# Operand placement, narrow projections in one tile, and 512-column units in a two-block forward pass on one core

## The chip, the cores and the metric

The kernel runs on one core of a Trainium2 chip. A core has TensorE (PE, matrix products), VectorE (DVE), ScalarE (ACT), GpSimd (POOL) and SyncE (SP, which here issues the loads); they run side by side and wait for one another through semaphores. The metric is the time of one execution on the device, in microseconds, as the median of several runs.

## The reference

A forward pass over 512 tokens of width 1024 in fp32: two layers of a first block (a mixer with a gated delta rule and HGRN2, then a convolutional FFN), then one layer of a second block (four mixers, one of them sparse attention, with gates, then an MLP). Cut to what this change touches:

```python
def _mixer(h, w_in, ...):                        # twice
    p = h @ w_in                                 # 1024 -> 6672 columns
    (qkv, z, beta_r, a_r, hq, hf_fwd, hf_bwd, hi, hgate, gate_dn, gate_hg) = _split(p, IN_SIZES)
    beta = jax.nn.sigmoid(beta_r) ...            # beta_r, a_r: 8 columns each, a "narrow projection"
    g = -jnp.exp(dn_a_log) * jax.nn.softplus(a_r + dn_dt_bias)
    ...
    for d, fr in enumerate((hf_fwd, hf_bwd)):    # 512 columns each: the decays
        logf = jax.nn.log_sigmoid(fr) + jnp.log1p(lb[d] * jnp.exp(-fr))
        kk = (1.0 - lb[d]) * jax.nn.sigmoid(-fr)
    ...
    return merged @ w_out
# second block, once
    (gu, gv, q, kc, vc, ks_, vs_, kw, vw, ng, ca, cb, sB, sC, sh) = jnp.split(xn @ w_in[l], split_points)
    ...                                          # ng: 12 columns, the other narrow projection
    gates = jax.nn.sigmoid(xn @ w_gate[l] + b_gate[l])
```

## The kernel before, in words

Every large product is made from three fp32r matmuls. An operand x is kept as a high part (x rounded to fp32r by ScalarE, HHI or WHI) and a low part (x minus the high part, HLO or WLO), and `product` adds high x high, low x high and high x low in PSUM for each tile k of 128 rows of the contraction (lines 145 to 147). A matmul loads 128 x 128 stationary elements and moves up to 512 columns past them.

Stages follow each other, each a block with a barrier, an own order written out by hand for each engine and waits on named steps. Per layer of the first block: `qkv_stage`, `delta_stage`, `hgrn_proj_stage` (called the decays' stage below), `hgrn_stage`, `branch_stage`, `out_and_ffn_stage`; then once `mixers_in_stage` (the mixers' projections), `attention_gate_stage` (the attention stage) and `out_and_ffn_stage` again as the MLP. In the trace they begin at about 22, 142, 267, 393, 508 and 649 us, the second layer at 1055, and the last three at 2087, 2270 and 2559.

In most projections a weight tile of 128 columns is stationary and the 512 tokens move. In the decays' stage the first three groups (g = 0, 1, 2: two decays and HGRN's values) come out with tokens on the partitions: 128 tokens (HHI, HLO) are stationary and weight columns move. A group of 512 columns is loaded and split in two units s of 256 columns and all eight tiles k (`Feed`, `token_quads`), so each matmul moves 256 columns into half a PSUM bank. A unit's steps are: SP loads RAW; ScalarE rounds it to WHI (`split_hi`, L193); VectorE subtracts into WLO (`split_lo`, L197); PE multiplies (4 token tiles c x 8 k x 3). At the stage's head nothing else is there for PE to do. Behind unit (0,0) PE makes four column sums of squares HSQ for a norm (L1224), whose buffer has two places; VectorE scales each into HR (the means, L1303) and splits the next two units after all four.

The narrow projections use `product` with 16 or 12 weight columns: 24 matmuls of 512 moving tokens each, into PS[0:16]. VectorE copies the result to BAT (or CB), and PE turns it by four transposes (L513).

In `out_and_ffn_stage` the eight weight tiles of w_out come first. The low part of tile 1 is made by VectorE (L2125), those from tile 2 on by GpSimd (L2188).

`new(name, shape, dtype, align)` places a buffer at a multiple of `align` bytes in each partition, 128 unless told otherwise. In the built program HHI begins 1408 bytes past a multiple of 2048 everywhere but in the FFNs and the MLP, and the weights WHI 1664 bytes past it in `qkv_stage`, 384 in the decays' stage, 1408 in `branch_stage`, 256 in the mixers' projections and the attention stage, and 0 in the FFNs and the MLP, where HHI is at 0 as well.

## Time and profile before

| | before |
|---|---|
| median of 3 runs | 2964.24 us (2963.05 to 2968.63) |
| the profiled execution | 2960.97 us, span 2959.2 us, mean granted clock 0.98 |
| PE | 2815.0 us busy, 95% of the span, 17694 matmul records |
| PE's weight loads | 2319.2 us, 78%, beside the matmuls |
| VectorE, ScalarE, GpSimd | 1488.1, 1179.8 and 972.9 us busy |
| HBM | 79 GB/s over the span |

Busy time of PE is the union of its matmuls. They overlap (a 512-column one lasts 0.39 us and the next starts 0.227 us later), so the distance from start to start says what a matmul costs, not its duration. A row with "[idle <- X]" tells that the engine stood before this instruction, and what ended that. The granted clock is TensorE's, 1.00 for 2.4 GHz and 0.50 for 1.2 GHz.

### The profile page before, as it was taken

What the parts mean: (1) busy time and instruction counts of PE and PEld (TensorE: products, weight loads), DVE (VectorE), ACT (ScalarE), POOL (GpSimd) and SP (SyncE); (2) the same over time, 40 slices, a digit from 0 to 9 for tenths busy, and PEclk for the clock granted to TensorE, in tenths of its full rate; (3) what the DMA queues carried; (4) which work ended last, traced back from release to release, by engine and by line L of the source; (5) the groups of instructions that cost most, each with busy time, mean ns of one, the idle gap of its engine ahead of it and who ended that gap; (6) DMA issues with size and microseconds to landing.
All of it is one profiled execution on the core that took longest, in us unless ns stands there. A gap on an engine that the chain in (4) does not pass through costs nothing. (4 is left out here: it accounts for less than half of the span.)

```text
span 2959.2 us, 42579 instructions
## 1 busy us (share of the span) xinstructions
PE 2815.0 (95%) x17694; PEld 2319.2 (78%) x17694; DVE 1488.1 (50%) x2068; ACT 1179.8 (40%) x1870; POOL 972.9 (33%) x513
## 2 busy tenths in 40 slices
PE   7988998999999989989989999999899999999999
PEld 5788976878888867889778788888677767788887
DVE  5565556437616455655564376265585552531120
ACT  4563655333313235527553333132334652342231
POOL 1263021014534413630210244444272323344433
PEclk8999999999999999999999999999899999999999
DMA  5101202333423241022023334232432213333322
GB/s 168 52 8 58 84 1 73 87 108 99 118 75 102 69 115 57 3 71 72 2 72 96 111 93 120 73 105 59 124 86 63 72 54 89 95 99 93 100 86 78
DMA packets 420512, 235.91 MB, mean 80 GB/s; under 512 B 24052, under 2 KB 416866, under 8 KB 419682
## 3 DMA queue, kind: packets, MB, share of 16 engines
q1 hardware_dynamic: 419442, 233.18, 27.4%
q8 instruction: 141, 2.31, 0.3%
q14 instruction: 49, 0.40, 0.0%
q10 hardware_dynamic: 880, 0.02, 0.0%
HBM read 226.88 MB, written 6.29 MB: 79 GB/s over the span
## 5 line engine op out<-in xcount | busy, mean ns | idle before, releaser
L2188 POOL TENSOR_TENSOR WLO<-RAW,WHI 128x1024 fp32r<-128x1024 f32 (+1 forms) x202 | 528.9, 2625 | 963.7 <-ACT WHI L2027 963.7
L145 PE MATMUL PS<-HHI,WHI 128*128 128x512 f32 x1920 | 757.9, 395 | 3.6 <-DVE WLO L2857 2.2
L147 PE MATMUL PS<-HHI,WLO 128*128 128x512 f32 x1920 | 750.2, 391 | 0.0
L146 PE MATMUL PS<-HLO,WHI 128*128 128x512 f32 x1920 | 750.0, 391 | 0.0
L145 PEld LDWEIGHTS PS<-HHI,WHI 128*128 128x128 f32 x1920 | 361.4, 188 | 89.7 <-issue 7.4
L2027 ACT CAST WHI<-RAW 128x1024 fp32r<-128x1024 f32 (+1 forms) x202 | 221.6, 1101 | 514.0 <-PE PS L147 499.2
L146 PEld LDWEIGHTS PS<-HLO,WHI 128*128 128x128 f32 x1920 | 361.5, 188 | 78.4 <-issue 2.7
L147 PEld LDWEIGHTS PS<-HHI,WLO 128*128 128x128 f32 x1920 | 361.1, 188 | 77.3
L2177 DVE TENSOR_TENSOR X<-X,PS 128x512 f32<-128x512 f32 x48 | 33.0, 688 | 334.1 <-PE PS L147 334.1
L2160 DVE SCALAR_TENSOR_TENSOR ACC<-GP,PARS,ACC 128x512 f32<-128x512 f32 x88 | 163.1, 1853 | 3.1
L145 PE MATMUL PS<-MHI,WHI 128*128 128x512 f32 x384 | 150.6, 392 | 9.3 <-DVE LHID L2121 4.2
L2919 POOL TENSOR_TENSOR WLO<-RAW,WHI 128x1280 fp32r<-128x1280 f32 x31 | 91.3, 2946 | 198.2 <-ACT WHI L2802 198.2
L147 PE MATMUL PS<-MHI,WLO 128*128 128x512 f32 x384 | 149.6, 390 | 0.0
L146 PE MATMUL PS<-MLO,WHI 128*128 128x512 f32 x384 | 149.5, 389 | 0.0
L145 PE MATMUL PS<-WHI,HHI 128*128 128x256 f32 x448 | 129.7, 290 | 10.9 <-DVE WLO L197 10.7
L193 ACT CAST WHI<-RAW 128x1536 fp32r<-128x1536 f32 (+1 forms) x52 | 85.2, 1641 | 124.7 <-PE PS L147 101.9
L146 PE MATMUL PS<-WLO,HHI 128*128 128x256 f32 x448 | 128.4, 287 | 0.0
L147 PE MATMUL PS<-WHI,HLO 128*128 128x256 f32 x448 | 128.4, 287 | 0.0
L197 DVE TENSOR_TENSOR WLO<-RAW,WHI 128x1536 fp32r<-128x1536 f32 (+1 forms) x52 | 101.9, 1960 | 50.4 <-ACT WHI L193 49.3
L610 POOL TENSOR_TENSOR WLO<-RAW,WHI 128x1024 fp32r<-128x1024 f32 x24 | 57.6, 2415 | 182.0 <-ACT WHI L383 182.0
L2639 POOL TENSOR_TENSOR WLO<-RAW,WHI 128x1024 fp32r<-128x1024 f32 x20 | 81.5, 4094 | 107.2 <-ACT WHI L2300 107.2
L2153 DVE TENSOR_TENSOR GP<-PS,RS 128x512 f32<-128x512 f32 x44 | 30.4, 692 | 152.8 <-PE PS L147 128.0
(481 smaller groups left out, 5224.5 us busy)
## 6 DMA issues: line engine op xcount, KB each, us to landing
RAW<-in_w_up SPq DMA_DIRECT2D x88, 512.0 KB, 3.8
RAW<-in_w_in SPq DMA_DIRECT2D x82, 512.0 KB, 4.1
RAW<-in_w_mlp SPq DMA_DIRECT2D x64, 512.0 KB, 3.9
RAW<-in_w_down SPq DMA_DIRECT2D x32, 704.0 KB, 4.5
RAW<-in_w_in SPq DMA_DIRECT2D x20, 1024.0 KB, 5.3
RAW<-in_w_gate SPq DMA_DIRECT2D x32, 512.0 KB, 3.7
RAW<-in_w_out SPq DMA_DIRECT2D x24, 512.0 KB, 4.9
x_kept<-X SPq DMA_DIRECT2D x2, 2048.0 KB, 9.4
```

The costliest lines, as they stand in the source:

```text
L145: e.matmul(out, wh, xh, start=first and n == 0, stop=False)
L146: e.matmul(out, wh, xl, start=False, stop=False)
L147: last = e.matmul(out, wl, xh, start=False, stop=final and n == len(quads) - 1)
L193: self.hi_st.done(act.copy(self.hi[:, s], self.raw[:, s]), f"unit{s}")
L197: self.lo_st.done(dve.tensor_tensor(self.lo[:, s], self.raw[:, s], self.hi[:, s], ALU.subtract), f"unit{s}")
L610: pool.tensor_tensor(WLO[:, u % N], RAW[:, u % N], WHI[:, u % N], ALU.subtract).then_inc(lo_pool, 1)
L2027: ac.done(act.copy(slot(WHI, u), source(u)), f"hi{u}")
L2160: dv.done(dve.scalar_tensor_tensor(acc, gp[:, n:n + 512], tap(n), acc, ALU.mult, ALU.add), f"tap{n}_{i}")
L2177: dv.done(dve.tensor_tensor(X[:, m, :], X[:, m, :], PS[:, 6 + m % 2, :], ALU.add), f"x{g}_{m}")
L2188: pool.tensor_tensor(slot(WLO, u), source(u), slot(WHI, u), ALU.subtract).then_inc(lo_s, 1)
L2639: pool.tensor_tensor(WLO[:, u % N], RAW[:, u % N], WHI[:, u % N], ALU.subtract).then_inc(S["lo_pool"], 1)
L2919: pool.tensor_tensor(WLO[:, u % 3], RAW[:, u % 3], WHI[:, u % 3], ALU.subtract).then_inc(lo_s, 1)
```

## The change

Five edits.

1. Placement: the pair HHI, HLO of the second block, and WHI, WLO of the mixers' projections and of the attention stage, are placed at multiples of 2048 bytes. In the built program both then begin at 0 past such a multiple. Nothing moves in the first block: the decays' stage keeps 1408 and 384.
2. Narrow projections: high and low weights stand side by side in one tile (WB, 32 columns; WN, 24). `narrow_product` multiplies this tile with HHI and then HLO, 16 matmuls instead of 24, and leaves two partial results in PS[0:32], low x low now among them. Four fp32 multiplies by FOLD, a tile with two identities one above the other that VectorE makes, turn them and add the halves; they stand in place of the transposes.
3. Decays' units: for g < 3 a unit s is now four tiles k of all 512 columns (`half_k`), so each matmul moves 512 columns. The unit (0,0) is rounded, subtracted and multiplied one tile k at a time.
4. Means and low parts: two of the four HSQ sums stand behind unit (0,0), two behind unit (0,1). VectorE makes two means, the low part of (1,0), two means, the low part of (1,1).
5. In `out_and_ffn_stage` the low part of w_out's tile 2 is made by VectorE, behind its first addition into X; GpSimd starts with tile 3.


VectorE in the decays' stage, before, from the low part of unit (0,1) to the logarithms (WLO<-RAW,WHI is `split_lo`, HR<-PS a mean; OHG holds the bound):

```order
L197 TENSOR_TENSOR WLO<-RAW,WHI 128x2048
L1294 TENSOR_SCALAR OHG<-OHG 128x1024
L1296 RECIPROCAL OHG<-OHG 128x1024
L1298 TENSOR_SCALAR OHG<-OHG,SMALLS 128x1024
L1300 TENSOR_SCALAR OHG<-OHG 128x1024
L1303 TENSOR_SCALAR HR<-PS 128x512 x4
L197 TENSOR_TENSOR WLO<-RAW,WHI 128x2048 x2
L1312 TENSOR_TENSOR LF<-HQ,OHG 128x512 x2
```

The same stretch now, with the four quarters of unit (0,0) ahead of it:

```order
L1320 TENSOR_TENSOR WLO<-RAW,WHI 128x512 x3
L1322 TENSOR_TENSOR WLO<-RAW,WHI 128x512
L1327 TENSOR_TENSOR OHG<-HQ 128x1024
L205 TENSOR_TENSOR WLO<-RAW,WHI 128x2048
L1330 TENSOR_SCALAR OHG<-OHG 128x1024
L1332 RECIPROCAL OHG<-OHG 128x1024
L1334 TENSOR_SCALAR OHG<-OHG,SMALLS 128x1024
L1336 TENSOR_SCALAR OHG<-OHG 128x1024
L1339 TENSOR_SCALAR HR<-PS 128x512 x2
L205 TENSOR_TENSOR WLO<-RAW,WHI 128x2048
L1339 TENSOR_SCALAR HR<-PS 128x512 x2
L205 TENSOR_TENSOR WLO<-RAW,WHI 128x2048
L1348 TENSOR_TENSOR LF<-HQ,OHG 128x512 x2
```

The first low part has become four of 512 elements, and one low part has moved between the second and the third mean.

PE in the decays' stage, before, the end of unit (0,0) and the start of unit (0,1) (HSQ,C are the column sums):

```order
L145 MATMUL PS<-WHI,HHI 128x256
L146 MATMUL PS<-WLO,HHI 128x256
L147 MATMUL PS<-WHI,HLO 128x256
L1224 MATMUL PS<-HSQ,C 128x512 x4
L145 MATMUL PS<-WHI,HHI 128x256
L146 MATMUL PS<-WLO,HHI 128x256
L147 MATMUL PS<-WHI,HLO 128x256
```

And now:

```order
L145 MATMUL PS<-WHI,HHI 128x512
L146 MATMUL PS<-WLO,HHI 128x512
L147 MATMUL PS<-WHI,HLO 128x512
L1249 MATMUL PS<-HSQ,C 128x512 x2
L145 MATMUL PS<-WHI,HHI 128x512
L146 MATMUL PS<-WLO,HHI 128x512
L147 MATMUL PS<-WHI,HLO 128x512
```

Two of the four sums have moved behind the next unit, and each product writes 512 columns; it stands half as often.

VectorE at the head of the first FFN, now (before, the two additions into X stand next to each other):

```order
L2165 MEMSET GP 128x2
L2175 TENSOR_TENSOR X<-X,PS 128x512
L2181 TENSOR_TENSOR WLO<-RAW,WHI 128x1024
L2175 TENSOR_TENSOR X<-X,PS 128x512
L2131 SCALAR_TENSOR_TENSOR HLO<-X,PARS,HHI 128x512
```

The low part of 1024 elements between the additions was the first of GpSimd's row.

```diff
@@ -148,6 +148,14 @@
     return last
 
 
+def narrow_product(e, out, W, pair):
+
+    for k in range(8):
+        for j in range(2):
+            last = e.matmul(out, W[:, k, :], pair[j][:, k, :], start=k + j == 0, stop=k + j == 8)
+    return last
+
+
 class Early:
 
 
@@ -204,10 +212,16 @@
         c = slice(m * P, (m + 1) * P)
         return [(self.hi[:, s, k, c], self.lo[:, s, k, c], H[0][:, k - k0, :], H[1][:, k - k0, :]) for k in range(k0, k1)]
 
-    def token_quads(self, s, c, H):
+    def token_quads(self, s, c, H, ks=range(4)):
 
         t = slice(c * P, (c + 1) * P)
-        return [(H[0][:, k, t], H[1][:, k, t], self.hi[:, s, k, :], self.lo[:, s, k, :]) for k in range(8)]
+        hi, lo = half_k(self.hi, s), half_k(self.lo, s)
+        return [(H[0][:, 4 * s + k, t], H[1][:, 4 * s + k, t], hi[:, k, :], lo[:, k, :]) for k in ks]
+
+
+def half_k(buf, s):
+
+    return buf[:, s].rearrange("p k n -> p (k n)").rearrange("p (k n) -> p k n", n=512)
 
 
 def after_step(used, names):
@@ -335,13 +349,14 @@
     K, N, T = 8, 4, 16
     tiles = (4, 5, 6, 7, 0, 1, 2, 3, 8, 9, 10, 11, 12, 13, 14, 15)
     RAW, WHI, WLO = new("RAW", [P, N, K, P]), new("WHI", [P, N, K, P], F32R), new("WLO", [P, N, K, P], F32R)
-    WBA, WBH, WBL = new("WBA", [P, K, 16]), new("WBH", [P, K, 16], F32R), new("WBL", [P, K, 16], F32R)
-    CONV, BAT, BA, TMP = new("CONV", [P, 4, 512]), new("BAT", [16, 512]), new("BA", [P, 4, 16]), new("TMP", [P, 3, 32])
+    WBA, WB = new("WBA", [P, K, 16]), new("WB", [P, K, 32], F32R)
+    CONV, BAT, BA, TMP = new("CONV", [P, 4, 512]), new("BAT", [32, 512]), new("BA", [P, 4, 16]), new("TMP", [P, 3, 32])
     RS, EPS, WARM = new("RS", [P, 512]), new("EPS", [P, 1]), new("WARM", [P, 1])
+    FOLD = TMP[0:32, 0, 16:32]
     SQ = [S1[:, n, :] for n in range(4)] + [S2[:, n, :] for n in range(4)]
     TK = [S2[:, n, :] for n in range(4)]
     names = ("loaded0", "loaded1", "loaded2", "loaded3", "weights_hi", "weights_lo_dve", "weights_lo_pool", "tiles_done",
-             "wba_in", "wba_hi", "wba_lo", "eps_set", "warm", "x_sums", "x_root", "x_normed", "x_hi", "x_lo",
+             "wba_in", "wba_hi", "wba_lo", "fold", "eps_set", "warm", "x_sums", "x_root", "x_normed", "x_hi", "x_lo",
              "taps", "silus", "squares", "sums", "logs", "roots", "unit", "ba_done", "ba_kept", "ba_turned", "ba_back",
              "gates", "keys_turned", "keys_kept", "values_turned", "values_kept", "z_done")
...
@@ -505,12 +520,13 @@
                         if k == K - 1:
                             last.then_inc(used, 1)
                 pe.wait_ge(S["wba_lo"], 1)
-                product(pe, PS[0:16, 7, :], [(WBH[:, k, :], WBL[:, k, :], pair[0][:, k, :], pair[1][:, k, :]) for k in range(K)]).then_inc(S["ba_done"], 1)
+                narrow_product(pe, PS[0:32, 7, :], WB, pair).then_inc(S["ba_done"], 1)
                 dense(4)
                 pe.wait_ge(S["ba_kept"], 1)
                 pe.wait_ge(S["x_root"], 1)
+                pe.wait_ge(S["fold"], 1)
                 for c in range(4):
-                    last = pe.transpose(PS[:, 6, c * 16:(c + 1) * 16], BAT[0:16, tokens(c)], C[0:16, IDENT, 0:16])
+                    last = pe.matmul(PS[:, 6, c * 16:(c + 1) * 16], BAT[:, tokens(c)], FOLD, start=True, stop=True)
                 last.then_inc(S["ba_turned"], 1)
                 for i in range(5, 10):
                     dense(i)
@@ -571,10 +587,11 @@
                 for k in range(K - N + 1, K):
                     low_of_input(k)
                 dve.wait_ge(S["wba_hi"], 1)
-                dve.tensor_tensor(WBL[:, :, :], WBA[:, :, :], WBH[:, :, :], ALU.subtract).then_inc(S["wba_lo"], 1)
+                dve.tensor_tensor(WB[:, :, 16:32], WBA[:, :, :], WB[:, :, 0:16], ALU.subtract).then_inc(S["wba_lo"], 1)
+                dve.tensor_tensor(FOLD, C[0:32, IDENT, 0:16], C[0:32, IDENT, 16:32], ALU.add).then_inc(S["fold"], 1)
                 conv(0)
                 dve.wait_ge(S["ba_done"], 1)
-                dve.tensor_copy(BAT[0:16, :], PS[0:16, 7, :]).then_inc(S["ba_kept"], 1)
+                dve.tensor_copy(BAT[:, :], PS[0:32, 7, :]).then_inc(S["ba_kept"], 1)
                 conv(1)
                 conv(2)
...
@@ -1190,7 +1207,9 @@
                 sp.dma_start(reach, A["consts"][:, REACH:REACH + 2 * LEVELS, :]).then_inc(reach_in, 16)
                 for g in range(1, 5):
                     for s in range(2):
-                        feed.load(sp, g, s, [(feed.raw[:, s], wl[:, :, ds(HGRN_COL + order[g] * 512 + s * UNIT, UNIT)])])
+                        col = HGRN_COL + order[g] * 512
+                        feed.load(sp, g, s, [(half_k(feed.raw, s), wl[:, 4 * s:4 * s + 4, ds(col, 512)])] if g < 3 else
+                                  [(feed.raw[:, s], wl[:, :, ds(col + s * UNIT, UNIT)])])
 
             @block.gpsimd
@@ -1212,14 +1231,20 @@
 
                 for g in range(3):
                     for s in range(2):
-                        feed.ready(pe, g, s)
-                        for c in range(4):
-                            if s == 0:
-                                bank_free(g, c)
-                            last = product(pe, bank(g, c)[:, s * UNIT:(s + 1) * UNIT], feed.token_quads(s, c, pair))
+                        if (g, s) == (0, 0):
+                            for k in range(4):
+                                pe.wait_ge(piece_lo, k + 1)
+                                for c in range(4):
+                                    last = product(pe, bank(0, c), feed.token_quads(0, c, pair, range(k, k + 1)), first=k == 0, final=False)
+                        else:
+                            feed.ready(pe, g, s)
+                            for c in range(4):
+                                if s == 0:
+                                    bank_free(g, c)
+                                last = product(pe, bank(g, c), feed.token_quads(s, c, pair), first=s == 0, final=s == 1)
                         proj.done(last, f"unit{g}_{s}")
-                        if (g, s) == (0, 0):
-                            for h in range(4):
+                        if g == 0:
+                            for h in (2 * s, 2 * s + 1):
                                 pe.wait_ge(sq_s, h + 1)
                                 pe.matmul(bank(1, h), C[:, ONES, :], SQ[:, h % 2, :], start=True, stop=True).then_inc(sum_s, 1)
                 for g in (3, 4):
@@ -1233,7 +1258,10 @@
             @block.scalar
             def _(act):
                 feed.hi_st.open(act)
-                feed.split_hi(act, 0, 0)
+                act.wait_ge(feed.loaded[0], feed.landed(0, 0))
+                for k in range(3):
+                    act.copy(half_k(feed.hi, 0)[:, k, :], half_k(feed.raw, 0)[:, k, :]).then_inc(piece_hi, 1)
+                feed.hi_st.done(act.copy(half_k(feed.hi, 0)[:, 3, :], half_k(feed.raw, 0)[:, 3, :]), "unit0")
                 feed.split_hi(act, 0, 1)
                 for h in range(2):
                     act.activation(SQ[:, h % 2, :], O[:, h, :], ACT.Square).then_inc(sq_s, 1)
@@ -1286,7 +1314,15 @@
             @block.vector
             def _(dve):
                 feed.lo_st.open(dve)
-                feed.split_lo(dve, 0, 0)
+                raw, hi, lo = half_k(feed.raw, 0), half_k(feed.hi, 0), half_k(feed.lo, 0)
+                for k in range(3):
+                    dve.wait_ge(piece_hi, k + 1)
+                    dve.tensor_tensor(lo[:, k, :], raw[:, k, :], hi[:, k, :], ALU.subtract).then_inc(piece_lo, 1)
+                feed.hi_st.wait(dve, 0, "unit0")
+                dve.tensor_tensor(lo[:, 3, :], raw[:, 3, :], hi[:, 3, :], ALU.subtract).then_inc(piece_lo, 1)
+                dve.wait_ge(piece_lo, 4)
+                dve.sem_inc(feed.lo_st.sem, 1)
+                feed.lo_st.given += 1
                 dve.wait_ge(logits_in, 32)
                 dve.tensor_tensor(LB, logits[:, 0, :], logits[:, 1, :], ALU.subtract).then_inc(bound_s, 1)
                 feed.split_lo(dve, 0, 1)
@@ -1301,8 +1337,8 @@
                 for h in range(4):
                     dve.wait_ge(sum_s, h + 1)
                     dve.tensor_scalar(R[:, h, :], bank(1, h), 1.0 / P, 1e-6, ALU.mult, ALU.add).then_inc(mean_s, 1)
-                feed.split_lo(dve, 1, 0)
-                feed.split_lo(dve, 1, 1)
+                    if h % 2:
+                        feed.split_lo(dve, 1, h // 2)
                 dve.wait_ge(bound_s, 6)
                 for g in range(2):
...
@@ -2140,6 +2176,9 @@
                     if t:
                         x_low(t - 1)
                         square_sum(t - 1)
+                    else:
+                        after(dve, ac, "hi2")
+                        dv.done(dve.tensor_tensor(slot(WLO, 2), source(2), slot(WHI, 2), ALU.subtract), "lo2")
                 x_low(K - 1)
                 square_sum(K - 1)
                 after(dve, ac, "rs")
@@ -2183,7 +2222,7 @@
 
             @block.gpsimd
             def _(pool):
-                for u in range(2, U):
+                for u in range(3, U):
                     after(pool, ac, f"hi{u}")
                     pool.tensor_tensor(slot(WLO, u), source(u), slot(WHI, u), ALU.subtract).then_inc(lo_s, 1)
@@ -2201,13 +2240,13 @@
 
     K, N, taps, T2 = 8, 4, 31, range(2)
     par, conv = PAR[:, 0, :], PAR[:, 1, :]
-    WHI, WLO = new("WHI", [P, N, K, P], F32R), new("WLO", [P, N, K, P], F32R)
+    WHI, WLO = new("WHI", [P, N, K, P], F32R, 2048), new("WLO", [P, N, K, P], F32R, 2048)
     GU, GV, KC, CB = new("GU", [P, 2, 512]), new("GV", [P, 4, UNIT]), new("KC", [P, 4, 512]), new("CB", [P, 2, 512])
     ZP, SC, SP, SBB = new("ZP", [P, 2, 542]), new("SC", [P, 2, 512]), new("SP", [P, 2, 514]), new("SBB", [P, 2, 512])
...
@@ -2669,7 +2709,7 @@
 
 
     scale = D_HEAD ** -0.5
-    WHI, WLO = new("WHI", [P, 3, 10, P], F32R), new("WLO", [P, 3, 10, P], F32R)
+    WHI, WLO = new("WHI", [P, 3, 10, P], F32R, 2048), new("WLO", [P, 3, 10, P], F32R, 2048)
     (YH, YL), raw01 = y_pair, next_raw
     PR, PT = new("PR", [P, 1024]), new("PT", [P, 4, UNIT])
     SG, TMP = new("SG", [P, 2, 512]), new("TMP", [P, 512])
@@ -2929,7 +2969,7 @@
     with ExitStack() as top:
         with ExitStack() as mid:
             new = new_in(mid)
-            pair = split_pair(new)
+            pair = split_pair(new, align=2048)
             Y = new("Y", [P, 8, 512])
             b = {n: new(n, s) for n, s in dict(
                 Q=[P, 2, 512], K=[P, 2, 512], V=[P, 2, 512], NG=[P, 4, 12], KCM=[P, N_CMP], VCM=[P, P]).items()}
@@ -3043,7 +3083,7 @@
                 new_r = new_in(zs, "right")
                 Z = new_r("Z", [P, 4, 512])
                 first = HGRN_COL + HGRN_ORDER[0] * 512
-                hgrn_early = Early(signals, new_r, 8, UNIT, lambda raw, s: [(raw[:, s], w_in_l[:, :, first + s * UNIT:first + (s + 1) * UNIT])])
+                hgrn_early = Early(signals, new_r, 8, UNIT, lambda raw, s: [(half_k(raw, s), w_in_l[:, 4 * s:4 * s + 4, first:first + 512])])
                 with ExitStack() as dn:
                     new = new_in(dn)
                     x_kept = signals.lasting(f"x_kept{l}")
```

## Rows read from the trace of the kernel before

**Rows 1.** The page, part 1: busy us, share of the span, instructions.

```profile
PE 2815.0 (95%) x17694; PEld 2319.2 (78%) x17694; DVE 1488.1 (50%) x2068; ACT 1179.8 (40%) x1870; POOL 972.9 (33%) x513
```

**Rows 2.** Timeline of PE, decays' stage: start us, us, engine, line, op.

```profile
302.15 0.28 PE L145 MATMUL PS<-WHI,HHI 128*128 128x256 f32 x1
...
313.55 0.28 PE L147 MATMUL PS<-WHI,HLO 128*128 128x256 f32 x1
```

**Rows 3.** Timeline of PE, first FFN stage, 220 matmuls apart.

```profile
755.20 0.39 PE L147 MATMUL PS<-HHI,WLO 128*128 128x512 f32 x1
...
805.07 0.39 PE L145 MATMUL PS<-HHI,WHI 128*128 128x512 f32 x1
```

**Rows 4.** Timeline of PE, attention stage, 240 matmuls apart.

```profile
2484.06 0.40 PE L146 MATMUL PS<-HLO,WHI 128*128 128x512 f32 x1
...
2539.80 0.40 PE L146 MATMUL PS<-HLO,WHI 128*128 128x512 f32 x1
```

**Rows 5.** Groups by line, mixers' projections, 2127.8 to 2150: count, busy us, mean ns.

```profile
L146 PE MATMUL PS<-HLO,WHI 128*128 128x512 f32 x32 | 12.6, 394 | 0.0
```

**Rows 6.** Timelines of PE, ScalarE and VectorE, head of the decays' stage.

```profile
272.59 0.58 PE L145 MATMUL PS<-WHI,HHI 128*128 128x256 f32 x1 [5.37 <-DVE WLO L197]
...
273.18 0.41 PE L147 MATMUL PS<-WHI,HLO 128*128 128x256 f32 x1
...
275.10 0.41 PE L147 MATMUL PS<-WHI,HLO 128*128 128x256 f32 x1
...
268.31 3.70 ACT L193 CAST WHI<-RAW 128x2048 fp32r<-128x2048 f32 x2 [3.95 <-PEq L654]
...
270.24 2.29 DVE L197 TENSOR_TENSOR WLO<-RAW,WHI 128x2048 fp32r<-128x2048 f32 x1 [2.30 <-ACT WHI L193]
```

**Rows 7.** Groups by line, whole span: the matmuls that move CR.

```profile
L1439 PE MATMUL PS<-CR,hFH 128*128 128x512 f32 x128 | 52.9, 414 | 0.0
```

**Rows 8.** Timelines of ScalarE and VectorE: one tile each.

```profile
644.35 0.62 ACT L1742 CAST MHI<-R 128x512 fp32r<-128x512 f32 x1 [3.63 <-DVE R L1815]
...
645.00 0.69 DVE L1781 TENSOR_TENSOR MLO<-R,MHI 128x512 fp32r<-128x512 f32 x1 [0.69 <-ACT MHI L1742]
...
2099.09 1.22 DVE L2531 TENSOR_TENSOR WLO<-RAW,WHI 128x1024 fp32r<-128x1024 f32 x1
```

**Rows 9.** Timelines of PE and GpSimd, heads of FFN and MLP.

```profile
656.48 0.50 PE L145 MATMUL PS<-MHI,WHI 128*128 128x512 f32 x1 [0.81 <-POOL WLO L2188]
...
2567.71 0.50 PE L145 MATMUL PS<-YHI,WHI 128*128 128x512 f32 x1 [2.32 <-POOL WLO L2188]
...
2565.31 9.89 POOL L2188 TENSOR_TENSOR WLO<-RAW,WHI 128x1024 fp32r<-128x1024 f32 x4 [28.85 <-ACT WHI L2027]
```

**Rows 10.** Windows: us, then busy us of PE, PEld, DVE, ACT, POOL, then clock.

```profile
270.10:276.80 6.70, 4.21 (x19) 4.21 (x20) 5.06 (x3) 4.02 (x5) 0.52 (x1) 0.50 1.01 350
...
2564.00:2576.00 12.00, 9.68 (x43) 7.68 (x42) 4.90 (x5) 8.57 (x11) 10.69 (x5) 1.00 0.72 199
...
2150.00:2180.00 30.00, 29.87 (x158) 24.97 (x157) 30.00 (x44) 12.60 (x18) 25.27 (x7) 1.00 0.47 124
```

**Rows 11.** Timeline of PE, the column sums in the decays' stage.

```profile
288.82 1.98 PE L1224 MATMUL PS<-HSQ,C 128*128 128x512 f32 x4 [0.86 <-ACT HSQ L1245]
...
290.24 0.68 PE L145 MATMUL PS<-WHI,HHI 128*128 128x256 f32 x1
```

**Rows 12.** Timeline of VectorE, low part of unit (2,0).

```profile
321.65 2.28 DVE L197 TENSOR_TENSOR WLO<-RAW,WHI 128x2048 fp32r<-128x2048 f32 x1
```

**Rows 13.** Timeline of PE, narrow projection and its transposes.

```profile
60.09 0.39 PE L145 MATMUL PS<-HHI,WBH 128*16 128x512 f32 x1
...
61.94 0.40 PE L147 MATMUL PS<-HHI,WBL 128*16 128x512 f32 x1
...
67.72 0.42 PE L513 MATMUL PS<-C,BAT 16*128 16x16 f32 x4
```

**Rows 14.** Timeline of PE, mixers' projections, the wait for ScalarE.

```profile
2211.84 1.19 PE L2463 MATMUL PS<-Y,C 128*128 128x512 f32 x1 [6.38 <-ACT SC L2358]
```

25 lines of the change are left out of this document (13 added, 12 removed).

## The prediction

> **What bounds the kernel now.** I read the page first: TensorE (PE) is busy 95% of the span [rows 1]. So a removed microsecond counts where the other engines wait for PE, and is lost where PE itself waits. Next I read PE's timeline as start-to-start distances between matmuls. Three pitches appear. With a moving operand of 256 columns, 95 steps take 11.40 us, 120.0 ns each [rows 2]. With 512 columns in the first FFN stage, 220 steps take 49.87 us, 226.7 ns each [rows 3]. The same kind of matmul in the attention stage takes 55.74 us for 240 steps, 232.2 ns [rows 4]; the mixers' projections have them at a mean duration of 394 ns [rows 5], 5 above the 0.39 us of rows 3. VectorE, ScalarE and GpSimd run beside all of these stages, so their traffic does not set the slow ones apart; where the operand tiles begin does. Last I read what ends PE's waits at each place that is changed.
>
> **The change part by part.** Savings are reckoned against the profiled execution, 2961.0 us (span 2959.2 and 1.8 around it).
>
> *Decays' units, 512 columns.* In each of two layers 576 matmuls of 256 columns become 288 of 512. A pair costs 240.0 ns now, a joined one 226.7 if this operand behaves as in rows 3: 13.3 ns saved. At half clock the 256-column pitch is 1.92 us / 9 = 213 ns [rows 6], all of it columns, and joining saves nothing; that concerns some 20 matmuls at the stage's head. So 278 x 13.3 ns = 3.7 us per layer, 7.4 in all. The trace does not show a 512-column moving tile at this place. Lower bound: 226.7 ns. Upper bound: the matmuls that move CR, with a mean duration of 414 ns [rows 7] where rows 5 have 394; 20 to 25 ns more over 576 are 14 us, and the edit would cost 6. I take 226.7, because the 256-column halves lie in the same buffer now and step evenly by 120.
>
> The Trainium skill has a rule that speaks against this edit: "TensorE: Matmul & The Clock Gate", section "Back-to-back issue gap", gives columns / 2.4 GHz plus about 2.5 ns. By that, joining would save 556 x 2.5 ns = 1.4 us. Rows 2 and 3 leave 13.3 ns over the columns' time (120.0 - 106.7, 226.7 - 213.3), so the measurement decides for the larger saving.
>
> *The stage's head.* PE is idle 5.37 us before 272.59, while ScalarE rounds 2048 elements (from 268.31, the first of two alike at 3.70 us) and VectorE subtracts as many (from 270.24) [rows 6]. Now a quarter goes first. For 512 elements ScalarE takes 0.62 and VectorE 0.69 us [rows 8], so PE starts at 268.31 + 0.62 + 0.03 + 0.69 + 0.05 = 269.70: 2.9 us earlier, 5.8 in two layers. Later quarters come every 0.7 us and PE needs 12 x 0.227 = 2.7 us for each, so it does not wait again.
>
> *The clock there.* The granted clock was 0.50 from 270.1 to 276.8, behind this idle stretch; it was 1.00 through the 12 us that hold PE's idle 2.32 us before 2567.71 [rows 9, 10]. The new idle stretch is 2.5 us, near the short one. If the clock stays full, the 4.2 us that PE now works at half speed give 2.1 us back. If it falls to half until the same moment, 7.1 us are worked at half speed instead, and 1.4 of the 2.9 us are lost. I take the middle, +0.4 us per layer, 0.8 in all, with -2.8 and +4.3 as ends.
>
> *Means and low parts.* Two of the four column sums move behind the second unit, and VectorE alternates. PE's wait of 0.86 us for HSQ goes [rows 11], since ScalarE has squares 3 and 4 long before. In its place comes a second change from fp32 sums to fp32r products, whose first matmul lasts 0.68 instead of 0.28 us [rows 2, 11]. Net 0.4 us per layer, 0.8 in all. On VectorE the third mean now waits for a sum behind the second unit; queued behind it is only the low part of unit (1,1), wanted ten microseconds later. The critical one is that of unit (2,0): ready at 323.93 [rows 12], wanted at 302.15 + 192 x 0.12 = 325.19. Its chain on ScalarE starts when the second unit ends (301.8) and takes 22.2 us. From that moment PE now has 23.4 us of work, and will have two sums (1.7) and two units (10.9 each), 23.5. The slack of 1.3 us stays.
>
> *Narrow projections.* At three places 24 matmuls become 16. The pitch is (61.94 - 60.09) / 8 = 0.231 us [rows 13], so 1.85 us each. The fold costs four fp32 multiplies of 16 columns instead of four transposes that took 0.42 us [rows 13]; below: nothing more; above: 8 passes at the 0.43 us of the HSQ sums' 512 columns, 3.4 us. I take 0.3, since the transposes have the same columns. Two places: 3.1 us. At the third, in the mixers' projections, PE waits 6.38 us later on, and VectorE is busy 30.00 of 30 us ahead of that [rows 10, 14], so these 1.5 us are swallowed, and so is the new placement's gain on tiles 4 to 15.
>
> *Operand places.* In the attention stage 984 matmuls of 512 columns come from 232.2 to 226.7 ns: 5.4 us. In the mixers' projections the first four tiles count (64 matmuls at full clock) and six dense tiles behind the wait (144): 208 x 5.5 ns = 1.1 us. VectorE's added FOLD stands before its chain begins and costs nothing there. Bounds: nothing, or 6.5 us.
>
> *Low part of w_out's third tile.* GpSimd ends PE's idle 0.81 and 2.32 us; it took 2.47 us for each tile [rows 9], VectorE takes 1.22 [rows 8]. The first wait goes whole, also in the second layer; of the third 1.2 us go: 0.8 + 0.8 + 1.2, and with the restart after a wait (0.50 us for the first matmul instead of 0.39) 3.0 us. Behind it on VectorE stands the second addition into X, at most 1 us late; the rounding of HHI waits for that, and PE needs HHI only after six more tiles.
>
> Sum: 7.4 + 5.8 + 0.8 + 0.8 + 3.1 + 5.4 + 1.1 + 3.0 = 27.4 us. The profile's 2961.0 would become 2933.6. The runs' median lies 3.2 us above the profile, so the forecast is 2964.2 - 27.4 = 2936.8 us.
>
> **Rivals.**
> 1. *Placement is not the cause of 232.* The slow stages also use other helpers. Against it: two slow stages with different company agree [rows 4, 5]. Price 6.5 us: 2943. Chance 0.10.
> 2. *Joining saves no fixed part.* If the part beyond the columns' time grows with the tile's width here, the 7.4 us are lost: 2944. Against it: rows 3, where a 512-column matmul carries the same 13.3 ns as a 256-column one. Chance 0.05. By the rule of the Trainium skill named above it would be 2943; the trace does not agree with its 2.5 ns.
> 3. *Another chain takes over in the decays' stage.* The slack is 1.3 us on unit (2,0) and some 2.6 on (2,1). If the alternation makes ScalarE's logarithms 3 us late, 2 to 4 us per layer come back: 2941 to 2945. Chance 0.08.
> 4. *Slower than before: the joined matmul.* Its moving tile is 2 KB wide and does not begin at a multiple of 2048. Each nanosecond of pitch costs 0.58 us. At CR's extra of 25 ns the kernel takes 2951, still faster; from 227 + 48 = 275 ns on it is slower than before, and at the 430 ns of an HSQ pass it takes over 3050. Chance 0.02 beyond the turning point, 0.04 for about 2951.
> 5. *The clock gives more.* Full clock at both heads makes 2933; if other pauses lose their half-clock stretches too, 2929. Chance under 2932: 0.08.
>
> **How the numbers follow.** The forecast case, 2932 to 2941, has 0.63; rivals 1 to 3, 2941 to 2946, 0.23; rival 4 0.06; under 2932 0.08. Eight in ten, with a little of each side, lie from 2929 to 2947. About 0.2% (6 us) is what a measurement of this kernel can tell from no change. Faster by more is everything under 2958: 0.95. Within it 0.02, several small losses together. Slower 0.03, rival 4 and a wait that no row shows.
>
> **What would show it.** In the profile after: a pitch of 226.7 ns in the decays' first three projections and in the attention stage; PE idle about 2.5 us at the decays' head, with the granted clock beside it; no wait for HSQ; a wait of 8 to 10 us where rows 14 have 6.38; no wait for w_out's third tile in the FFNs, and one of 1.1 us in the MLP. A decays' pitch over 232, an attention pitch still at 232, or a wait of PE for VectorE between the decays' units would make the forecast wrong.

## The result and the profile after

The changed kernel takes 2940.44 us (median of 4 runs, 2931.62 to 2943.49) beside 2966.09 us for the kernel before in the same session (4 runs): a ratio of 0.9912, 95% interval 0.9900 to 0.9923. The forecast was 2936.8 us. Run again beside other kernels it took 2936.52 us (5 runs, 2935.74 to 2942.50), ratio 0.9921 [0.9908, 0.9933]. The profiled execution is 2943.49 us long, its span 2941.7 us.

The page of the changed kernel, part 1, which answers to [rows 1]:

```profile
PE 2803.8 (95%) x17106; PEld 2296.1 (78%) x17106; DVE 1494.4 (51%) x2080; ACT 1180.8 (40%) x1876; POOL 966.0 (33%) x510
```

TensorE has 588 records fewer and 11.2 us less of busy time, so part of the 17.5 us between the two profiles is idle time that went. Its timeline in the decays' stage, with 90 matmuls between the two rows (compare [rows 2]):

```profile
300.03 0.39 PE L145 MATMUL PS<-WHI,HHI 128*128 128x512 f32 x1
...
320.43 0.39 PE L145 MATMUL PS<-WHI,HHI 128*128 128x512 f32 x1
```

That is 20.40 us / 90 = 226.7 ns for a joined matmul, where two halves took 240.0. The wait of 0.86 us for HSQ [rows 11] is gone. In the attention stage, 240 matmuls apart (compare [rows 4]):

```profile
2460.09 0.39 PE L147 MATMUL PS<-HHI,WLO 128*128 128x512 f32 x1
...
2514.49 0.39 PE L147 MATMUL PS<-HHI,WLO 128*128 128x512 f32 x1
```

54.40 us / 240 = 226.7 ns, and no longer 232.2. The mixers' projections, as groups by line from 2117.8 to 2140 (count, busy us, mean ns; compare [rows 5]), went the same way:

```profile
L146 PE MATMUL PS<-HLO,WHI 128*128 128x512 f32 x31 | 12.1, 390 | 0.0
```

The head of the decays' stage, timelines of PE, ScalarE and VectorE (compare [rows 6]):

```profile
266.92 0.80 PE L145 MATMUL PS<-WHI,HHI 128*128 128x512 f32 x1 [2.50 <-DVE WLO L1320]
...
265.52 1.66 ACT L1263 CAST WHI<-RAW 128x512 fp32r<-128x512 f32 x3 [3.96 <-PEq L671]
...
266.17 2.08 DVE L1320 TENSOR_TENSOR WLO<-RAW,WHI 128x512 fp32r<-128x512 f32 x3 [1.03 <-ACT WHI L1263]
```

PE's idle time is 2.50 us in place of 5.37, and it starts 0.75 us after VectorE does, when the first quarter is there. The row of the mixers' wait (compare [rows 14]):

```profile
2201.25 3.75 PE L2502 MATMUL PS<-Y,C 128*128 128x512 f32 x4 [6.72 <-ACT SC L2397]
```

Laying the two profiles side by side, stage by stage (from a stage's first matmul to the next one's), shows where time went and where it came back. In the hgrn stage (the gated recurrence of HGRN2, behind the decays') no instruction was changed:

| stage, us | before | after | difference |
| --- | --- | --- | --- |
| input projections, layers 1 and 2 | 119.08, 118.28 | 117.56, 118.26 | -1.5, 0.0 |
| delta rule with the decays' head | 131.02, 129.76 | 126.38, 126.47 | -4.6, -3.3 |
| decays' projections | 120.29, 120.29 | 115.13, 115.16 | -5.2, -5.1 |
| hgrn | 113.15, 113.13 | 117.52, 117.63 | **+4.4, +4.5** |
| branches | 136.62, 136.64 | 138.21, 136.53 | +1.6, -0.1 |
| FFN | 412.70, 415.37 | 411.58, 415.13 | -1.1, -0.2 |
| mixers, attention, MLP | 179.89, 290.91, 394.99 | 179.14, 286.95, 392.39 | -0.8, -4.0, -2.6 |

What the delta rule's row of layer 1 has beyond the head (1.8 us) and the +1.6 of its branches go with the clock: the time at half clock there fell from 12.8 to 3.5 us and rose from 2.9 to 6.2. The view of windows tells the hgrn stage's 8.9 us. Its columns are window, length, then busy us of PE, PEld, DVE, ACT, POOL, the granted clock, DMA share and GB/s. First the stage in both layers of the kernel before, then of the changed kernel, then the changed kernel's 5 us with a pause and the two stretches behind it:

```profile
392.88:506.03 113.15, 95.89 (x1296) 80.61 (x1297) 78.77 (x187) 59.97 (x120) 30.23 (x24) 0.97 0.07 19
1423.67:1536.80 113.13, 95.89 (x1296) 80.66 (x1297) 78.81 (x187) 59.97 (x120) 30.23 (x24) 0.97 0.07 18
```

```profile
382.05:499.58 117.53, 100.27 (x1297) 84.62 (x1297) 79.32 (x187) 60.52 (x120) 30.22 (x24) 0.92 0.07 18
1409.26:1526.89 117.63, 100.44 (x1296) 84.65 (x1297) 79.44 (x187) 60.58 (x120) 30.23 (x24) 0.93 0.07 18
...
395.00:400.00 5.00, 2.70 (x71) 2.21 (x71) 4.17 (x7) 2.26 (x5) 2.68 (x2) 1.00 0.00 0
400.00:403.40 3.40, 3.40 (x41) 3.28 (x39) 3.40 (x12) 0.59 (x1) 0.00 (x0) 0.50 0.03 5
403.40:407.00 3.60, 3.60 (x44) 2.83 (x43) 2.87 (x10) 2.23 (x5) 0.00 (x0) 1.00 0.00 0
```

The same 1296 matmuls are busy 4.4 us longer, at a granted clock of 0.92 in place of 0.97. Half clock (0.50 of full speed, the 1.2 GHz level) comes here in stretches of 3.4 or 6.8 us behind pauses of TensorE. The changed kernel has three in each hgrn stage that the profile before has not, behind pauses that both have: the one before 399.83 is 2.52 us long from start to start, its twin in the kernel before (its end is at 410.71) 2.51 us, with the clock at 1.00 behind it.

### The profile page after: what moved, and what is told of

It is laid out like the page before. It is cut to its first block and busy times, and to the rows that moved or that the text cites. A ratio compares the mean times of both kernels' runs of the same rounds, so it can differ in the third digit from the quotient of the medians.

```text
span 2941.7 us, 41421 instructions
## 1 busy us (share of the span) xinstructions
PE 2803.8 (95%) x17106; PEld 2296.1 (78%) x17106; DVE 1494.4 (51%) x2080; ACT 1180.8 (40%) x1876; POOL 966.0 (33%) x510
## 3 DMA queue, kind: packets, MB, share of 16 engines
q8 instruction: 137, 2.24, 0.3%
## 5 line engine op out<-in xcount | busy, mean ns | idle before, releaser
L2227 POOL TENSOR_TENSOR WLO<-RAW,WHI 128x1024 fp32r<-128x1024 f32 (+1 forms) x199 | 521.9, 2629 | 967.5 <-ACT WHI L2063 967.5
L145 PE MATMUL PS<-WHI,HHI 128*128 128x512 f32 (+1 forms) x256 | 96.4, 377 | 7.3 <-DVE WLO L1320 5.1
L145 PE MATMUL PS<-YHI,WHI 128*128 128x512 f32 x256 | 100.5, 393 | 1.4 <-DVE WLO L2161 1.2
L147 PE MATMUL PS<-YHI,WLO 128*128 128x512 f32 x256 | 99.8, 390 | 0.0
```

Source lines behind the costliest of these rows:

```text
L145: e.matmul(out, wh, xh, start=first and n == 0, stop=False)
L147: last = e.matmul(out, wl, xh, start=False, stop=final and n == len(quads) - 1)
L2227: pool.tensor_tensor(slot(WLO, u), source(u), slot(WHI, u), ALU.subtract).then_inc(lo_s, 1)
```

## Experiments

**Each part alone.** Four kernels, each the kernel before with one part of the change. The places: `new("WHI", [P, N, K, P], F32R)` and its fellows get `, 2048`, and the second block's pair HHI, HLO `align=2048`; nothing else.

> The kernel before with the three places of the weight tiles alone (mixers, attention's projections start at multiples of 2048 bytes). Theory (place sets the pitch of the matmuls): attention's pitch falls from 232.2 ns to about 227 and the mixers' from 232.5 to about 227, time -5 to -7 us (5.4 + 1.1 us of the forecast's sum). Rival (the place is not the cause): both pitches stay at 232 and the time is within 1 us of before; then the pitch of after comes from another part of the change.

Measured: ratio 0.9987 [0.9978, 0.9996], so -3.9 us (-1.2 to -6.5). The attention stage in its profile, again 240 matmuls apart:

```profile
2480.06 0.39 PE L145 MATMUL PS<-HHI,WHI 128*128 128x512 f32 x1
...
2534.46 0.39 PE L145 MATMUL PS<-HHI,WHI 128*128 128x512 f32 x1
```

226.7 ns with nothing changed but where the tiles begin: rival 1 is out. The attention stage is 3.9 us shorter and the mixers' 0.8, as in the changed kernel. The 5 to 7 us that were expected are not reached, neither by these two stages (4.8) nor by the runs. In the profile even that is hidden, by 3.0 us more in the first hgrn stage and 2.0 in the MLP. This kernel's code in the hgrn stage is that of the kernel before, and yet:

```profile
390.14:506.28 116.14, 98.89 (x1296) 83.14 (x1296) 79.21 (x187) 60.46 (x120) 30.26 (x24) 0.94 0.07 18
1427.17:1540.30 113.13, 95.90 (x1296) 80.67 (x1296) 78.81 (x187) 59.97 (x120) 30.22 (x24) 0.97 0.07 19
```

Two layers of one execution, same instructions, 3.0 us apart by the clock alone.

The decays' part alone (joined units, quarters at the head, sums and means in turn):

> The kernel before with the decays' part alone (units of 512 columns, first unit in four quarters, sums and means taking turns with the low parts). Theory: the pieces shown by after's trace stay with this part: -5.1 us a layer of decays' matmuls, -2.9 us a layer at the head, and the half-clock stretches in the stage behind cost back 4 us a layer if they depend on this part: -8 to -15 us. If the clock's loss in the stage behind depends on where in time the pauses fall, as I hold, it can be there or not in each run, and the profiled run's granted clock goes with the time: a step of 3.4 us at half clock for each 1.7 us of time. Rival (the joined matmuls save only in after's places): -3 us or less.

Measured: 2950.37 us, ratio 0.9950 [0.9938, 0.9963], -14.8 us; the decays' projections took 115.20 us in both layers (-5.1 each), the head's pause was 2.77 and 2.86 us from start to start, and the hgrn stages took 117.80 and 117.83 with 17.6 us each at half clock. The theory holds: this part brings more than half of the gain, and the loss in the stage behind does not need the other parts. (Nor does it need this one: in the kernels with the narrow projections alone and with the third low part alone, below, three of the four hgrn stages took 116.1 to 116.6 us.)

To see what the quarters do, the same kernel with the first unit whole:

```diff
-                            for k in range(4):
-                                pe.wait_ge(piece_lo, k + 1)
-                                for c in range(4):
-                                    last = product(pe, bank(0, c), feed.token_quads(0, c, pair, range(k, k + 1)), first=k == 0, final=False)
+                            feed.ready(pe, 0, 0)
+                            for c in range(4):
+                                last = product(pe, bank(0, c), feed.token_quads(0, c, pair), first=True, final=False)
```

> The kernel before with the decays' part as in the run of that part alone, but the first unit's two halves of K undivided: ScalarE casts 2048 elements, VectorE subtracts 2048, and only then does TensorE begin. Theory (the quarters shorten the head by having TensorE start after 512 elements of each): the pause ahead of the first matmul of the decays' stage is 2.8 to 3.0 us longer than with quarters (5.7 us, as in the kernel before), and the time 5.5 to 6 us longer than that run's. Rival (the pause with quarters is short for another reason, such as the joined unit's own order): the pause stays at 2.8 us.

Measured: 2955.30 us, ratio 0.9972 [0.9963, 0.9981], 6.5 us more by the ratios (4.9 by the medians). Its first matmul:

```profile
271.57 0.80 PE L145 MATMUL PS<-WHI,HHI 128*128 128x512 f32 x1 [5.38 <-DVE WLO L197]
```

The pause is back at 5.38 us, while the projections stayed at 115.13 and 115.61 us: the joined units and the quarters are two separate gains.

The narrow projections alone (16 matmuls in place of 24, one fold matrix), and the third low part alone (`lo2` on VectorE, GpSimd's loop from 3):

> The kernel before with the narrow projections alone, in three places. Theory: 8 passes of 512 columns less in each (16 matmuls in place of 24: 8 x 227 ns = 1.8 us), less what a wait behind it swallows: -2 to -4.6 us, most likely -3. Rival: each is swallowed by the wait behind it, within 1 us of before.

> The kernel before with the third low part of the output weights on VectorE alone. Theory: the wait for the third tile at the head of the two FFN stages and of the MLP goes (0.8 us and 2.3 us in the profile of before, and GpSimd's chain behind it is one tile shorter): -2 to -4 us. Rival: VectorE's own work at the head comes later by the 1.2 us of the added instruction and TensorE waits for that in place of the weights: 0 to +3 us.

Measured: 0.9987 [0.9978, 0.9996] and 0.9987 [0.9979, 0.9996], -3.9 us each by the ratio, 3.4 and 2.8 by the medians. In its profile the narrow projections' kernel has the first place 2.1 us shorter, the second 0.5, the third 0.3, so most of one place and little of two. Over more profiles the first two come out larger: without the new projection (5 profiles) the input stages took 118.26 to 119.50 and 118.25 to 119.43 us, with it (6 profiles without fills there) 117.03 to 117.56 and 117.45 to 118.31. By the middle ones that is 1.9 and 0.6 us. The third low part makes FFN, FFN and MLP 1.1, 0.6 and 1.0 us shorter; in the MLP TensorE still waits 1.29 us, now for VectorE's low part. Neither rival held. The four parts' differences of medians, -2.5, -12.9, -3.4 and -2.8, sum to -21.6 us, by the ratios to -26.5. The whole change has -25.7 and -24.8 in its two sessions by the medians, -26.1 and -23.4 by the ratios. So the parts add up about as far as this can be measured; that one of them takes a few us from another would not be seen in this.

**Is it the clock?** The changed kernel once more, and a version in which TensorE has matmuls of no use in the three pauses of each hgrn stage:

```diff
                 def level(m, d, n):
+                    if n == 2 and m < CH - 1:
+                        pe.wait_ge(S["ac"][d], m * (LEVELS - 1) + 1)
+                        for _ in range(3 if m == CH - 2 else 0 if d else 7):
+                            for h in H4:
+                                for rows in HALVES:
+                                    pe.matmul(small(d, 2)[rows, h, :], kt_of(m, d)[:, h, rows], q_of(m, d)[:, h, rows], start=True, stop=True)
                     pe.wait_ge(S["x"][d], 2 * (m * LEVELS + n + 1))
```

> The changed kernel once more, unaltered, beside the next three. Theory (where the half-clock stretches of the gated recurrence's stage fall is chance, and they make the distance between the forecast and the measured time): the median stays at 2938 to 2942 us, some of the runs have a granted clock of 0.983 or more and are 5 to 10 us shorter than the rest, and the stage takes 110.2 us + 0.42 us for each us at half clock, as in the six profiles so far (111.6 us with 3.4 at half clock, 113.1 with 7.3, 116.1 with 14.3, 117.5 with 17.7). Rival (the change itself makes the stage longer): 117.5 us in both layers again with another time at half clock.

> The changed kernel with matmuls of no use (64x64, fp32, 36 ns each) in TensorE's three pauses of 2.5, 2.45 and 1.55+1.28 us in the gated recurrence's stage, before chunks 1, 2 and 3 are prepared: 56, 56 and 24+24 of them, into a region of PSUM that the next real matmuls overwrite. Theory (a pause there halves the clock for 3.4 us in some runs, and that is what the stage lost): the pauses stay where they are, no half-clock stretch begins at them, the stage is 113.1 to 113.7 us in both layers in place of 117.5, and the time falls by up to 8.8 us against the changed kernel's usual runs. Rival (the clock's stretches are not tied to the pauses): the stage keeps 14 to 18 us at half clock, or it grows by the fill where a pause was shorter than it (up to 1 us each).

Measured for the changed kernel: 2936.52 us. Three runs had a granted clock of 0.981 or 0.982 (2935.7 to 2936.5 us), two 0.980 and 0.979 (2939.5 and 2942.5), and in the first session the one with 0.983 took 2931.62 against 2940 to 2943 at 0.978 and 0.979. I had expected a median of 2938 to 2942 us and the better runs, at 0.983 or more, 5 to 10 us below the rest; the median was lower, no run reached 0.983, and the better ones were 3 to 7 below (9 to 12 in the first session). The profiled one was of the long kind, and its hgrn stages took 117.36 and 117.62 us again, so it does not tell the two theories apart by itself.

The fills say more. Measured: 2933.89 us (4 runs, 2931.4 to 2934.2), ratio 0.9905 [0.9892, 0.9919], 2.6 us under the changed kernel beside it. PE's timeline at the first pause, and the windows of the two stages:

```profile
397.08 3.44 PE L1495 MATMUL PS<-HQ,RAW 128*64 128x64 f32 x112
400.34 2.04 PE L1506 MATMUL PS<-hX 128*64 128x64 f32 x64
...
382.70:495.29 112.59, 102.26 (x1616) 87.92 (x1616) 78.92 (x187) 59.93 (x120) 30.31 (x24) 0.98 0.07 19
1403.62:1518.62 115.00, 104.91 (x1616) 90.10 (x1616) 79.01 (x187) 60.45 (x120) 30.47 (x24) 0.96 0.07 19
```

The real matmuls start 4.24 us after the levels ahead of the pause begin (396.10), where it was 4.38 us without fill (395.45 to 399.83), so the pause has its length. But no half-clock stretch begins at a filled pause in either layer; the stages are 4.8 and 2.6 us shorter, the second at 115.0 us outside the 113.1 to 113.7 expected. What is left begins at pauses that were not filled. (The fills had 56 matmuls recorded as 112; they took 3.4 us and not 2.0, which just fitted.) The rival would have had the stretches stay. One profile is weak evidence, since the profile before has no stretch at these pauses either, without any fill. Stronger is that all four runs have a granted clock of 0.983 or 0.984, where eight of the nine runs of the changed kernel have 0.978 to 0.982; and the kernels below with fills at eight more places have 0.993 to 0.995 in all nine runs.

The hgrn stages of the nine kernels that leave its code alone take 111.6 us with 3.4 at half clock to 118.0 with 17.5. A straight line through the 18 stages has a price of 0.43 us for each us at half clock and misses none of them by more than 0.5. The medians differ by 2.6 us only and the two profiles' spans by 8.4 (2940.7 and 2932.3), since most of the changed kernel's other runs had a higher clock than the profiled one.

**Why TensorE pauses there.** Timelines of PE, VectorE and GpSimd in the changed kernel, the first of the three pauses:

```profile
399.83 1.90 PE L1500 MATMUL PS<-hX 128*64 128x64 f32 x32 [2.30 <-DVE hX L1644]
...
397.00 1.38 DVE L1643 TENSOR_TENSOR hX<-HQ,X 128x256 f32<-128x256 f32 x1
398.30 1.48 DVE L1644 TENSOR_TENSOR hX<-RAW,X 128x256 f32<-128x256 f32 x1
399.70 0.41 DVE L1643 TENSOR_TENSOR hX<-HQ,hE 128x256 f32<-128x256 f32 x1
...
396.82 2.68 POOL L1423 TENSOR_TENSOR hFL<-LF,hFH 128x512 fp32r<-128x512 f32 x2 [8.14 <-ACT hFH L1572]
```

VectorE's instruction of 256 elements takes 0.41 us, and 1.38 and 1.48 while GpSimd subtracts: each waits for about one of GpSimd's two instructions of 1.34 us. So the subtraction was moved to VectorE, to a place where TensorE has other work:

```diff
-                    if m + 1 < CH:
-                        for d in lanes:
-                            low(m + 1, d)
...
                             for d in lanes:
                                 gather(m, d, n)
+                        if n == 2 and m + 1 < CH:
+                            for d in lanes:
+                                dve.wait_ge(S["fh"][d], m + 2)
+                                dve.wait_ge(S["g"][d], 8 * (m + 1))
+                                dve.tensor_tensor(B[d]["FL"][:, :], LF[:, row(m + 1, d), :], B[d]["FH"][:, :], ALU.subtract).then_inc(S["fl"][d], 1)
```

> The changed kernel with the low parts of the log decays of chunks 1 to 3 on VectorE, after the third level's gather, in place of GpSimd. Theory (in each of those pauses two VectorE instructions of 128x256 take 1.38 and 1.48 us in place of 0.41 while GpSimd subtracts 128x512 twice, 2.68 us: the two engines stand in each other's way, and TensorE waits for it): these instructions take 0.41 us again, the three pauses fall below 1 us, -4 to -6 us a layer by themselves and up to 4.3 us a layer of half clock: -8 to -20 us against the changed kernel. Rival (VectorE's chain is the bound, and 2 x 0.69 us more on it for each chunk come back as waits): within 3 us of the changed kernel or up to 4 us slower.

Measured: 2921.79 us (2921.43 to 2923.46), ratio 0.9868 [0.9852, 0.9883], 14.7 us under the changed kernel. The same place in its profile, PE and VectorE:

```profile
396.95 1.36 PE L1497 MATMUL PS<-hX 128*64 128x64 f32 x32 [0.26 <-DVE hX L1641]
...
396.15 0.41 DVE L1640 TENSOR_TENSOR hX<-HQ,X 128x256 f32<-128x256 f32 x1
396.48 0.42 DVE L1641 TENSOR_TENSOR hX<-RAW,X 128x256 f32<-128x256 f32 x1
...
398.15 1.28 DVE L1679 TENSOR_TENSOR hFL<-LF,hFH 128x512 fp32r<-128x512 f32 x2
```

The idle time is 0.26 us and the hgrn stages take 107.46 and 108.74 us, with 7.8 and 6.8 us at half clock in place of 17.7 and 17.5. By the price above the clock is some 9 of the 18.8 us that the two stages lost in the profiles, the pauses themselves the rest (an estimate from these numbers). The 1.28 us of work that VectorE took over cost nothing.

The Trainium skill, "SBUF — State Buffer", section "Who interferes with whom", says that a VectorE instruction with two inputs in SBUF and a GpSimd instruction that reads SBUF exclude each other, whichever comes first holding the other up for its whole length. The trace agrees: 1.38 and 1.48 us in place of 0.41, and 0.41 again once GpSimd is silent.

**The same idea in the mixers' stage, and it fails.** There 32 additions of 62 columns take 21.3 us of VectorE's chain, since seven of them last 2.4 us in place of 0.26 beside GpSimd. Made into four:

```diff
-                    for j in range(16):
-                        src = KC[:, 2 * t:2 * t + 2, 2 * j:2 * j + 16 * (N_CMP - 1) + 1:16]
-                        dst = CW[:, t, j, :].rearrange("p (h n) -> p h n", h=KV)
-                        dv.done(dve.tensor_scalar(dst, src, par[:, PE_ + 16 * t + j:PE_ + 16 * t + j + 1], None, ALU.add), f"cw{t}_{j}")
+                    for j in T2:
+                        src = KC[:, 2 * t:2 * t + 2, 16 * j:16 * j + 16 * N_CMP].rearrange("p h (n r) -> p h n r", r=16)[:, :, :, 0:16:2].rearrange("p h n r -> p r h n")
+                        ...
+                        dv.done(dve.tensor_tensor(dst, src, emb, ALU.add), f"cw{t}_{j}")
```

> The changed kernel with the 32 additions of 62 columns that make the compressed windows (mixers' stage) as 4 of 496 columns. Theory (VectorE's chain ends TensorE's waits of 7.3 and 2.6 us in that stage, and 8 of the 32 additions take 2.4 us in place of 0.26 while GpSimd subtracts): VectorE needs some 5 us in place of 21.3 us for them, both waits go or shrink below 1.5 us, and the half-clock stretches behind them too: -6 to -11 us. Rival (what TensorE waits for hangs on ScalarE's or GpSimd's chain): within 2 us of the changed kernel.

Measured: 2937.56 us (4 runs), ratio 0.9916 [0.9903, 0.9930]: no gain, and in the profile the mixers' stage is 2.8 us longer (182.00 for 179.18). VectorE and PE did what the theory says, up to a point. First VectorE's and GpSimd's timelines of the changed kernel (its second profile), then VectorE, GpSimd and PE of this one:

```profile
2137.34 11.82 DVE L2547 TENSOR_SCALAR CW<-KC,PARS 128x62 f32<-128x62 f32 x16
...
2151.32 15.43 POOL L2679 TENSOR_TENSOR WLO<-RAW,WHI 128x1024 fp32r<-128x1024 f32 x3 [2.98 <-ACT WHI L2339]
```

```profile
2131.72 1.93 DVE L2548 TENSOR_TENSOR CW<-KC,PARS 128x496 f32<-128x496 f32 x2
...
2122.38 34.20 POOL L2680 TENSOR_TENSOR WLO<-RAW,WHI 128x1024 fp32r<-128x1024 f32 x4 [3.01 <-ACT WHI L2339]
...
2122.38 25.81 POOL L2680 TENSOR_TENSOR WLO<-RAW,WHI 128x1024 fp32r<-128x1024 f32 x1 [3.01 <-ACT WHI L2339]
...
2148.24 0.80 PE L145 MATMUL PS<-HHI,WHI 128*128 128x512 f32 x1 [10.29 <-POOL WLO L2680]
```

VectorE needs 3.8 us for the additions, and TensorE's wait of 6.72 us ahead of L2502 shrinks to 1.99 (7.3 and 2.6 from start to start). But now VectorE works without a gap on long instructions from 2122 to 2146. GpSimd's four subtractions, 2.4 us each when alone, take 34.2 us; the row of the window 2140 to 2147 shows that the first of them takes 25.81 of these, until VectorE slows down, and the three behind it 2.8 each. TensorE waits 10.29 us for that first one. In the changed kernel (its second profile again) the same subtraction takes 11.72 us:

```profile
2128.00 11.72 POOL L2679 TENSOR_TENSOR WLO<-RAW,WHI 128x1024 fp32r<-128x1024 f32 x1 [3.00 <-ACT WHI L2339]
...
2137.34 2.45 DVE L2547 TENSOR_SCALAR CW<-KC,PARS 128x62 f32<-128x62 f32 x1
```

It ends with the first slow addition, at 2139.7. So the slow small additions were the places where GpSimd got on. The four large ones differ from them in kind as well (tensor_tensor in place of tensor_scalar), and which of the two matters was not tried. My theory saw one half of this sharing, the rival named the right engine.

**Fills at the other pauses.** With the subtraction on VectorE as base, fills at eight more places, six of them `pe.matmul(out, C[:, ONES, :], C[:, ONES, :], start=True, stop=True)`, n times, into a bank that the next real matmul overwrites, and two in the last chunk of the hgrn stage with 32 small ones as above:

> The changed kernel with the low parts of chunks 1 to 3 on VectorE, and matmuls of no use in TensorE's other longer pauses: at the head of the projections (20 and 30 of 128x128, fp32) and of the mixers (30), ahead of the delta rule's first level (24), at the heads of the decays' and the branches' stages (8, 12), before the sum over the convolution's result (42), and in the last chunk of the gated recurrence (32 + 32 of 64x64). Theory (half clock follows the pauses, and costs 0.42 us for each us): of the 99.6 us at half clock in the run of the first edit alone some 50 go, and the time falls by 10 to 20 us against it, 2921.8 us. Rival (a fill that is too long delays the real work, or the clock falls all the same): no gain, or up to 10 us slower, where the fills were run at half clock and outlast their pause.

Measured: 2923.16 us, ratio 0.9867 [0.9853, 0.9880], clock 0.993: the half clock fell from 99.6 to 42.5 us, as the theory has it, and the time did not, as the rival has it. A fill's row in the mixers' head shows why (30 matmuls, recorded as 60):

```profile
2051.28 6.86 PE L154 MATMUL PS<-C 128*128 128x128 f32 x60
2057.90 0.95 PE L2490 MATMUL PS<-HHI,WHI 128*128 128x512 f32 x3
```

One takes some 230 ns where I had reckoned 140. So the real work behind them starts 0.2 to 1.5 us later than without fills, and the 42 of them stood at a place without a pause: the mixers' stage is 9.7 us longer. Cut and moved:

> The kernel of the run before it with its fills cut to their pauses: the fills' matmuls took 230 ns each and not the 140 ns I had reckoned with, so that they ended 0.5 to 2 us after what TensorE waited for (24 -> 15 ahead of the delta rule's levels, 30 -> 26 and 24, 20 -> 18, 12 -> 8, 8 -> 6), and the 42 that stood where there was no pause (9.7 us) are now 25 in the 7.3 us pause ahead of the third of the queries' and keys' sums. Theory (the fills give back the half clock's price where they do not outlast the pause): 9.7 us and 7 us of overlap go, the mixers' stage loses 3 us of half clock: 2903 to 2909 us against 2923.2, and 13 to 19 us under the version without fills (2921.8). Rival (busy fills cost what they give): 2914 us or more.

Measured: **2906.88 us** (5 runs, 2905.84 to 2907.51), ratio 0.9812 [0.9799, 0.9826]. This is the fastest version, 54 us under the kernel before it ran beside and 30 to 34 under the changed kernel. Both hgrn stages without any half clock:

```profile
379.49:484.99 105.50, 99.08 (x1441) 83.44 (x1441) 76.01 (x193) 59.97 (x120) 21.97 (x18) 1.00 0.08 20
1390.36:1496.25 105.89, 99.07 (x1440) 83.43 (x1440) 75.92 (x193) 59.96 (x120) 22.39 (x18) 1.00 0.08 20
```

35.1 us of the execution are left at half clock, of 127.1. It gained 14.9 us over its base for 64.5 us less half clock, about half of what 0.43 would give. Stage by stage the price differs: the input projections have 4.6 and 6.9 us less at half clock and are 1.1 and 0.2 us longer than in the base, so half clock seems to cost nothing there. (The first of them takes 117.03 us without any in the kernel with the narrow projections alone, and 117.03 with 13.8 us of it in that with the four additions.) At the mixers' head the real work still starts 1.1 us late.

## Why the forecast came out as it did

The forecast was right within 4 us of the first median and within 1 of the second. Its steps, by profile and experiments:

- *Joined units, 7.4 us, with the sums' 0.8 and the clock's 0.8*: measured -5.16 and -5.13 us in the stage. The pitch of 226.7 ns gives the 7.4; what is left, 2.9 us, is 1.3 more than the two small terms, and what that is was not looked for. TensorE has no wait over 0.3 us behind the first matmul of the stage. Rivals 2, 3 and 4 are out, and so is the Trainium skill's 2.5 ns from "TensorE: Matmul & The Clock Gate", section "Back-to-back issue gap": 226.7 ns are 13.4 over the columns' time at 512 columns too.
- *The head, 5.8 us*: the pause went from 5.65 to 2.77 us start to start (5.66 and 2.77 without and with quarters, in the two experiments) and in layer 2 to 2.86, 2.9 and 2.8: right.
- *The clock, +0.8 with ends at -2.8 and +4.3*: right at the head itself, where the half-clock stretch is 3.4 us long (266.84 to 270.25) in place of 6.8. Wrong in scope. I looked at the clock at the changed places alone; the sign that it can fall elsewhere stood in rival 5, but with a gain only. In the profiled run it cost 8.9 us in the hgrn stages.
- *Operand places, 5.4 and 1.1 us*: 4.0 and 0.8. The pitch came out as forecast. The first term was mis-sized by 1.4 us: 984 x 5.5 ns counts every matmul of the stage at 232.2 ns, as those between the rows that I had taken. The fifth or so of them that move YHI or YLO stepped by 229.4 to 230.4 ns on the mean and had less to gain; that leaves part of the 1.4 us open.
- *Narrow projections, 3.1 us at two places*: 1.5 and 0.0 in the profile, 2.1 and 0.5 in the part's own. The first place held. At the second the head of the stage waits 6.81 us for ScalarE's HHI in place of 5.36, which is a change ahead of this edit; nothing I ran tells why. That wait is 5.23 to 6.15 us in the kernels without the new projection, so the one profile before, at the low end, makes this place look worse than the 0.6 us over all profiles do. The third place was swallowed, as forecast: PE's wait there is 6.72 us.
- *Third low part, 3.0 us*: the waits for it at the first FFN and the MLP are gone, that of the second FFN is 0.90 us from 1.20 start to start: 4.0 us in the stages, of which the part alone brought 2.7. In the MLP I had expected 1.1 us of wait to stay; it is gone in the changed kernel, and 1.29 us in that of this part alone. Without the edit GpSimd's wait there is anything from 0.62 to 2.69 us, so the one profile before says little of its size.
- *The wait of 8 to 10 us in the mixers' stage*: it is 6.72 us, and a second one of 2.2 us for GpSimd's low part stands 38 us ahead of it. The sum is as forecast, its place is not: GpSimd and VectorE hold each other up there.

The forecast's terms without the clock are 26.6 us, and as measured above they are about as much (10.3 + 5.7 + 4.8 + 1.5 + 4.0 = 26.3, a little clock at the head included). The medians of the runs moved by 25.7 and 24.8, the two profiles by 17.5 only. The difference is the hgrn stages: the profile before had 7.3 and 7.2 us of half clock there, and other executions of the same code had 14.3 and 17.6. Adding a sum of terms to the median, and not to the one profile, is what kept the forecast near. That part was luck as much as method: had the median fallen on runs such as the profiled one, 2943.5 us, the forecast would have been 7 us off, for a reason that none of its rivals had.

Why are equal pauses followed by half clock in one execution and not in another? In every one of the 13 profiles the changes of the granted clock lie on an even raster of time, to within 0.02 us, and against the start of the program this raster lies elsewhere in each execution. In the 18 hgrn stages with unchanged code the pause's place on the raster separates the cases without an exception. At the first pause (the one that ends at 399.83 in the changed kernel and at 410.71 in the kernel before) half clock follows in the 11 stages where the next point of the raster comes at most 1.1 us behind the pause's end, in one of them 0.1 us ahead of it, and not in the 7 where it comes 2.1 to 3.0 us behind. At the second it follows in 11 with 1.26 to 1.70 us and not in 7 with 1.74 to 2.24. The Trainium skill, "TensorE: Matmul & The Clock Gate", section "What's actually happening", describes a monitor of TensorE's activity that runs by a clock of its own, not by the program's; by that the same pause would count at one moment and not at another. The traces agree: two layers of one execution had 14.3 and 7.2 us at half clock. This is read from traces; no run here moved a pause and nothing else.

## What to carry to other kernels

Before a small gain is booked, look at the granted clock in the stages that the change does not touch: identical instructions took 111.6 to 118.0 us here, so two single profiles can be 9 us apart over nothing, and medians of several runs have to carry the verdict. Where TensorE pauses some 2 us again and again, ask first what VectorE and GpSimd do to each other just then: moving one subtraction off GpSimd was worth 14.7 us, as much as the largest part of this change. The other way round, many small instructions on VectorE can be what lets GpSimd get on, so merging them is no gain by itself. Where a pause cannot be removed, matmuls of no use in it keep the clock up, if they end before it does; their length is to be read from a trace first.

## What was not expected of the hardware

- Where the operand tiles begin sets the pitch of 512-column fp32r matmuls: 232.2 ns before, 226.7 ns with the weights' tiles and the pair HHI, HLO at multiples of 2048 bytes, nothing else changed. Multiples of 2048 are not what it takes: in the profile before, the input projections, the last two groups of the decays' and the branches step by 226 to 228 ns on the mean with HHI at 1408 and WHI at 1664, 384 and 1408 bytes past one. Only the stages with WHI at 256 were slow. Which of the addresses matters, and why, was not tried.
- VectorE and GpSimd: 128x256 tensor_tensor on VectorE 0.41 us, 1.38 to 1.48 beside GpSimd's tensor_tensor; 128x62 tensor_scalar 0.26 us, up to 2.48. The other way round, GpSimd's 128x1024 subtraction takes 2.41 us alone and 25.8 beside VectorE's uninterrupted 512-column instructions.
- Half clock costs 0.43 us for each us in a stage where TensorE is busy 85% of the time, and it comes behind pauses as short as 1.3 to 2.5 us, though not behind each. In these traces it went by the pause's moment, on a raster that does not start with the program.
- An fp32 matmul of 128x128 with its weights takes some 230 ns (30 in 6.86 us) and leaves two records; the row's count is of records, not of matmuls.
